# Two-block layer on one core: a modulation batch moved to the ends of the state space groups, and five changes of order in the second block

## The chip, the cores and the metric

The kernel runs on one core of a Trainium2 chip. The metric is the device time of one execution in microseconds; the time of a kernel is the median of its runs.

## The reference

One call computes two transformer-like blocks on a sequence of 256 positions with 2048 features, all in float32. The first block is modulated by a vector `c`: `silu(c) @ w_mod + b_mod` gives six vectors of 2048 that shift, scale and gate. Its mixer joins a dilated attention and a state space branch; then comes a SwiGLU part. The second block has three branches (a linear recurrence with gates, a compressed and windowed attention, an attention with forget gates) and merges them.

```python
mod = (c_act @ w_mod[l] + b_mod[l])[:, None, :]
sh1, sc1, g1, sh2, sc2, g2 = jnp.split(mod, 6, axis=-1)
h = rmsnorm(x, norm1_w[l]) * (1.0 + sc1) + sh1
x = x + g1 * mixer(h, ...)
h = rmsnorm(x, norm2_w[l]) * (1.0 + sc2) + sh2
x = x + g2 * swiglu(h, w_ffn_in[l], w_ffn_out[l])
...
a = jnp.exp(log_a)
drive = jnp.sqrt(-jnp.expm1(2.0 * log_a)) * (inp * uc.astype(jnp.float32))
_, hseq = lax.associative_scan(linear_combine, (a, drive), axis=1)
...
merged = (mg[:, :, 0] * (y_a @ w_branch[l, 0])
          + mg[:, :, 1] * (y_b @ w_branch[l, 1])
          + mg[:, :, 2] * (y_c @ w_branch[l, 2]))
```

## The kernel before

All large products go through TensorE as **chunks**: 16 weight tiles of 128x128 (1 MB), that is one tile of 128 output features over 2048 inputs. There are 544 chunks in one fixed order, in phases with names: `ple`, `qs`, `qkv`, `dt`, `gs`, `ssm0`, `sp0`, `ssm1`, `sp1`, `ap`, `ga`, `wo`, `fi`, `fo` for the first block, `lx`, `lg`, `bf`, `nq`, `cmp`, `bra`, `ng`, `fx`, `brb`, `fg`, `brc`, `w2`, `pg` for the second. `ga`+5 is the sixth chunk of phase `ga`, and `C0["ga"]` is the number of its first.

Every weight is split into an upper and a lower part so that float32 accuracy survives TensorE's reduced format. For chunk c, SyncE loads `raw[c % 4]` as soon as TensorE has used chunk c-4; ScalarE makes the upper half `whi` (line 1088, function `hi`), VectorE the lower half `wlo` (line 1610, function `lo`), both two chunks ahead of TensorE as a rule. TensorE multiplies each tile three times (upper by upper, upper by lower, lower by upper), either as three narrow matmuls of 256 columns (lines 513 to 515) or as one of 512 and one of 256 (508 to 511). Its result is fetched from the accumulator by ScalarE (`take`, line 1098, with an activation function) or VectorE (`add`, line 1620). Every engine runs its own program in the order of the text; only semaphores tie them.

**Modulation.** `w_mod` has 24 batches of 512 columns (order `MORDER`), each of four pieces of 1 MB. Batches from 8 on ride beside other phases by a table: `MPIECE` says after which chunk's load SyncE issues a piece, `MDVE` (two chunks earlier in number, at VectorE's place) when VectorE multiplies and adds it (`mod_piece`, four operations of 128x512, lines 1671 and 1673), `MSUM` after which chunk TensorE sums the batch over the partitions (`mod_block`, eight short matmuls, line 579, waits for `macc_ok`, which VectorE gives by a drain, line 1680), `MDONE` when VectorE adds the bias (`mod_finish`, line 1706). Before, two batches ride in each of `sp0`, `sp1` and `ga`, one in `wo`, four in `fi`.

**State space groups.** `ssm0` and `ssm1` have four groups of ten chunks each. At the end of a group VectorE finishes four tiles (`xs`, `sz`, lines 1964 and 1967) from the products that TensorE makes after the tenth chunk (line 790); ScalarE squares them (line 1298) and TensorE sums the squares (line 744) in the middle of the next chunk.

**Second block.** In `lx` the first four chunks (`leads`) are multiplied before the norm is known; then VectorE rebuilds the input in four quarters: `joined` (line 2204) adds upper and lower part, `normed` (line 2210) scales, ScalarE's `hi_quarter` makes the new upper part, `low_quarter` (line 1768) the new lower part, for which TensorE's next three chunks (`triple`) wait quarter by quarter. `lead_out` (lines 2193 and 2195) and the convolution (lines 2233 and 2236) follow. In `lg`, in two halves i = 0, 1, ScalarE takes eight gates with Silu, and between them Sigmoid, Tanh and Exp (lines 1464 and 1466) and a square root (line 1479) for the recurrence, in the shared buffers `lt` and `la`; a change of function can need a table load. In `bra` the products of the first branch are merged (`branch_post`) while the logits of the first attention batches begin (`att_logits`, line 994); they need `hn_ok`, which VectorE gives after the norm of the compressed keys (lines 1655 to 1659 and 2348). Batch b+1 of the logits waits until VectorE has the maximum of batch b (`att_bias`, line 2368, semaphore `aA`). In `ng` VectorE gates eight tiles (`gated`, lines 2405, 1638, 1640) and computes the forget gates' softplus and their running sum (lines 1719 to 1739, 2438). `brb` is the same as `bra` for the second branch, beside the attention with forget gates (`NSA_B` is its first batch, lines 994 and 997).

Of the kernel before, what the change touches and what calls it, by code (L numbers as in the profile page):

```python
# [12 lines left out]
P = 128  # L13
S = 256
# [59 lines left out]
def first_and_second_block(nc, w16, w11, wm, cst_d, onehot, xt, pt, wab, cw2, out):  # L74
    ctx = ExitStack()
    with ctx:
# [51 lines left out]
        macp = sb("macp", [P, 512], W + 100352)  # L128
        cz = sb("cz", [P, 16, 64], W + 69632)
# [74 lines left out]
        lt = sb("lt", [P, 4, S], W + 8192)  # L204
        LR, LI = ([sb(f"{n}{i}", [P, 4, S], W + o + (24576 if i else 0)) for i in range(2)] for n, o in (("lr", 0), ("li", 4096)))
        la = sb("la", [P, 4, S], W + 98304)
# [178 lines left out]
        MSTAGES = [(0, 13, mraw_a, 4), (13, 15, mraw_b, 4), (15, 17, mraw_b, 4), (17, 20, mraw_w, 2), (20, 24, mraw_c, 2)]  # L385
        MACC = {n: (macc, macp)[n % 2] for n in range(24)}
        MPIECE = {}
        for n0, c0, k, per in ((8, C0["qkv"] + 2, 20, 1.1), (13, C0["sp0"] + 4, 8, 1.4), (15, C0["sp1"] + 4, 8, 1.4), (17, C0["ga"] + 2, 8, 1.4),
                               (19, C0["wo"] + 2, 4, 2), (20, C0["fi"] + 10, 16, 4)):
            for i in range(k):  # L390
                MPIECE.setdefault(c0 + int(i * per), []).append(int(4 * n0) + i)
        MWAIT = {C0["sp0"] + 3: (grp, 5), C0["sp1"] + 3: (grp, 9), C0["fi"] + 3: (used, 2 * C0["fi"])}
        MDVE = {c - 2: ms for c, ms in MPIECE.items()}
        MLAST = {m // 4: c for c, ms in MDVE.items() for m in ms if m % 4 == 3}
        MSUM = {c + 1: n for n, c in MLAST.items()}
# [93 lines left out]
        def _(pe):  # L489
# [338 lines left out]
            for h in range(2):  # L828
# [7 lines left out]
                pe.wait_ge(mod_ok, 15 + 2 * h)  # L836
# [196 lines left out]
            def attention(b0, b1, ph):  # L1033
                att_logits(b0)
                for b in range(b0, b1):
                    if b + 1 < b1:
                        att_logits(b + 1)
                    rides = RIDES.get(b, [])
                    for n in rides[:-1]:
                        branch_chunk(ph, n)  # L1040
# [38 lines left out]
        def _(act):  # L1079
# [228 lines left out]
            for h in range(2):  # L1308
                if h:
                    act.wait_ge(mod_ok, 15)  # L1310
# [143 lines left out]
            for j in range(8):  # L1454
                i = j // 4
                lr, li = LR[i], LI[i]
                c, e = C0["lg"] + j, E0["lg"] + j
                hi(c + 2)
                if j % 4 == 2:
                    act.wait_ge(lru_g, i + 1)  # L1460
                    if i:
                        act.wait_ge(lru_y, 1)
# [5 lines left out]
                take(c, e, gl[:, j, :], ACT.Silu, bias=C("b2", B2["lg"] + j))  # L1468
# [134 lines left out]
        def _(dve):  # L1603
# [294 lines left out]
            def group(i, h, gg):  # L1898
# [25 lines left out]
                for j in range(10):  # L1924
# [8 lines left out]
                    if j < 6:  # L1933
                        convolve(j)
                    if j == 1 and g % 4:
                        norm_scale(g - 1).then_inc(y_sc, 1)
# [260 lines left out]
            def joined(m):  # L2197

                if m % 2:
                    dve.wait_ge(used, 2 * (C0["lx"] + 3) + m // 2 + 1)  # L2200
                else:
                    dve.wait_ge(lead_q, m // 2 + 1)
# [3 lines left out]
            def normed(m):  # L2206

                dve.drain()
                t = wide(m, 4)
                dve.tensor_tensor(accM[:, t, :], accM[:, t, :], wide_rstd, ALU.mult).then_inc(quarter, 1)  # L2210

            lo(C0["lx"] + 4)
            lead_out(0)
            lo(C0["lx"] + 5)
            joined(0)
            normed(0)
            for m in range(4):
                if m < 3:
                    joined(m + 1)
                low_quarter(8 + m, accM)  # L2220
                if m < 3:
                    normed(m + 1)
                if m == 0:
                    lo(C0["lx"] + 6)
# [24 lines left out]
            for i in range(2):  # L2249
                li = LI[i]  # L2250
# [93 lines left out]
            branch_post("a", 1)  # L2344
# [4 lines left out]
            dve.drain().then_inc(hn_ok, 1)  # L2349

# [73 lines left out]
            for t in range(8):  # L2424
                if t != 3:
                    split_lo(C0["ng"] + t + 1)
# [5 lines left out]
                if t == 2:  # L2432
                    split_lo(C0["ng"] + t + 2)
                    softplus(zf[f, :], [sft[f, k, :] for k in (0, 1, 2, 3)], sft[f, 4, :], 4, cut=False)
                    dve.tensor_scalar(sft[f, 4, :], sft[f, 4, :], -1.0, None, ALU.mult)
# [228 lines left out]
```

## Time and profile before

| | us |
|---|---|
| median of 3 runs | 3318.47 (3317.68 to 3318.89) |
| the profiled execution | 3317.84 |
| its span | 3316.0 |
| TensorE busy | 3222.9 (97%) |
| VectorE busy | 2285.1 (69%) |
| ScalarE busy | 1532.5 (46%) |

The page's chain that ended last is 81% TensorE, 9% VectorE, 3% DMA and 3% ScalarE. DMA moved 209 GB/s over the span. In a timeline row, the number in brackets is how long the engine was idle before the row, and what ended that.

### The profile page before, as it was taken

The numbers are of one execution on the slowest core, as the hardware profiler recorded it, in microseconds if no ns is written. First come the engines' busy times: TensorE is split into PE (matmuls) and PEld (weight loads), VectorE is DVE, ScalarE is ACT, GpSimd is POOL, SyncE is SP. The second block draws the span as 40 slices with busy tenths as digits, with TensorE's granted clock in tenths as the row PEclk, the third lists the DMA queues.
The fourth block names the chain that finished last, engine by engine and source line by source line (L and its number), as shares of the span: only waits on it lengthen the run. The fifth ranks groups of instructions, "written<-read, shape, count | busy, mean of one in ns | idle before, by whom it ended". The sixth has DMA issues, their size and how long they took to land.

```text
span 3316.0 us, 52301 instructions
## 1 busy us (share of the span) xinstructions
PE 3222.9 (97%) x22161; PEld 2948.0 (89%) x22161; DVE 2285.1 (69%) x2781; ACT 1532.5 (46%) x1555; POOL 0.2 (0%) x4
## 2 busy tenths in 40 slices
PE   6999999999999999999999999999899999999999
PEld 4888989988998898988888888889899999999987
DVE  5797478877777788777776556766555664555676
ACT  2333555644554334433333333466656474443433
POOL 0000000000000000000000000000000000000000
PEclk9999999999999999999999999999999999999999
DMA  9897545556455686566665566544533444455554
GB/s 374 327 351 271 197 174 182 185 225 234 178 178 193 252 305 241 204 233 236 223 234 200 184 204 202 182 170 170 212 132 139 154 171 147 153 182 210 206 186 157
DMA packets 110413, 693.02 MB, mean 209 GB/s; under 512 B 11519, under 2 KB 18751, under 8 KB 36324
## 3 DMA queue, kind: packets, MB, share of 16 engines
q1 hardware_dynamic: 97776, 655.30, 54.5%
q10 hardware_dynamic: 12404, 34.38, 2.8%
q8 instruction: 175, 2.87, 0.3%
q14 instruction: 58, 0.48, 0.0%
HBM read 679.05 MB, written 13.72 MB: 209 GB/s over the span
## 4 chain that ended last, share of the span: by engine, by line
PE 81%; DVE 9%; DVEq 3%; DMA 3%; ACT 3%; issue 1%; ACTq 0%; SPq 0%
PE accp L508 25%; PE accp L509 14%; PE accp L513 10%; PE accp L515 10%; PE accp L514 10%; DVE wlo L1610 2%; DMA raw<-w 2%; PE accp L511 1%; DVEq L1675 1%; ACT whi L1088 1%; PE pw L589 1%; DVE macc L1673 1%; DVE macp L1673 1%; PE pw L994 1%; PE pw L1029 1%
## 5 line engine op out<-in xcount | busy, mean ns | idle before, releaser
L1610 DVE TENSOR_TENSOR wlo<-raw,whi 128x2048 fp32r<-128x2048 f32 (+1 forms) x544 | 1201.7, 2210 | 530.2 <-ACT whi L1088 525.4
L1088 ACT ACTIVATE whi<-raw 128x2048 fp32r<-128x2048 f32 (+1 forms) x544 | 1002.5, 1847 | 621.0 <-DMA raw<-w 588.5
L508 PE MATMUL accp<-act,whi 128*128 128x512 f32 x2550 | 908.7, 399 | 1.8 <-DVE tf L1620 0.9
L513 PE MATMUL accp<-act,whi 128*128 128x256 f32 x2912 | 844.1, 290 | 12.3 <-ACT gl L1098 5.4
L514 PE MATMUL accp<-act,whi 128*128 128x256 f32 x2912 | 827.9, 284 | 0.0
L515 PE MATMUL accp<-act,wlo 128*128 128x256 f32 x2912 | 827.8, 284 | 0.0
L509 PE MATMUL accp<-act,wlo 128*128 128x256 f32 x2720 | 734.7, 280 | 0.0
L513 PEld LDWEIGHTS accp<-act,whi 128*128 128x128 f32 x2912 | 562.8, 193 | 21.4 <-issue 7.4
L508 PEld LDWEIGHTS accp<-act,whi 128*128 128x128 f32 x2550 | 478.9, 188 | 112.2 <-DVE tf L1620 1.2
L514 PEld LDWEIGHTS accp<-act,whi 128*128 128x128 f32 x2912 | 563.0, 193 | 5.2 <-issue 5.0
L515 PEld LDWEIGHTS accp<-act,wlo 128*128 128x128 f32 x2912 | 562.6, 193 | 0.0
L509 PEld LDWEIGHTS accp<-act,wlo 128*128 128x128 f32 x2720 | 513.1, 189 | 14.7
L508 PE MATMUL accp<-hid,whi 128*128 128x512 f32 x688 | 243.7, 399 | 0.0
L509 PE MATMUL accp<-hid,wlo 128*128 128x256 f32 x704 | 195.1, 281 | 0.0
L508 PE MATMUL accp<-y,whi 128*128 128x512 f32 x450 | 161.7, 401 | 5.0 <-DVE accS L1634 1.8
L508 PEld LDWEIGHTS accp<-hid,whi 128*128 128x128 f32 x688 | 129.3, 188 | 31.4
L1306 ACT ACTIVATE tf<-tf 128x256 f32<-128x256 f32 x42 | 17.6, 418 | 258.3 <-DVE tf L1620 252.0
L509 PEld LDWEIGHTS accp<-hid,wlo 128*128 128x128 f32 x704 | 133.0, 189 | 1.5
L509 PE MATMUL accp<-y,wlo 128*128 128x256 f32 x480 | 129.9, 281 | 0.0
L1098 ACT ACTIVATE tm<-accp,cst 128x256 f32<-128x256 f32 x64 | 30.4, 475 | 183.4 <-PE accp L515 183.2
L513 PE MATMUL accp<-yb,whi 128*128 128x256 f32 x384 | 111.2, 290 | 0.0
L514 PE MATMUL accp<-yb,whi 128*128 128x256 f32 x384 | 109.8, 286 | 0.0
(503 smaller groups left out, 4191.9 us busy)
## 6 DMA issues: line engine op xcount, KB each, us to landing
raw<-w SPq DMA_DIRECT2D x480, 1024.0 KB, 4.8
raw<-w SPq DMA_DIRECT2D x64, 704.0 KB, 4.1
mraw_a<-wm SPq DMA_DIRECT2D x42, 1024.0 KB, 8.6
mraw_b<-wm SPq DMA_DIRECT2D x16, 1024.0 KB, 8.4
mraw_c<-wm SPq DMA_DIRECT2D x16, 1024.0 KB, 6.9
mraw_w<-wm SPq DMA_DIRECT2D x12, 1024.0 KB, 7.0
mraw_x<-wm SPq DMA_DIRECT2D x10, 1024.0 KB, 15.7
acb<-ac_d ACTq DMA_DIRECT2D x8, 1024.0 KB, 4.6
```

What stands on the lines that cost most here:

```text
L508: pe.matmul(acc, wh, both, start=first, stop=False, skip_group_check=True)
L509: mm = pe.matmul(acc[:, 0:S], wl, x2[:, 0, :], start=False, stop=False, skip_group_check=True)
L511: mm = pe.matmul(acc, wh, both, start=first, stop=True, skip_group_check=True)
L513: pe.matmul(acc[:, 0:S], wh, x2[:, 0, :], start=first, stop=False)
L514: pe.matmul(acc[:, 0:S], wh, x2[:, 1, :], start=False, stop=False)
L515: mm = pe.matmul(acc[:, 0:S], wl, x2[:, 0, :], start=False, stop=last)
L589: mm = pe.matmul(pw[64 * (k % 2):64 * (k % 2) + 64, 0, :], cz[:, 4 * j + k, :], mod_slot(4 * n + j)[:, k, :], start=j == j0 and k < 2, sto ...
L994: mm = pe.matmul(o, qq, kk, start=True, stop=kind != 3)
L1029: mm = pe.matmul(o, l, x, start=opens and r == 0 and t == 0, stop=kind >= 2 and t == q and r == 3, skip_group_check=True)
L1088: act.activation(whi[:, c % 4, 0:k, :], raw[:, c % 4, 0:k, :], ACT.Copy).then_inc(hi_done, 1)
L1610: dve.tensor_tensor(wlo[:, c % 4, 0:k, :], raw[:, c % 4, 0:k, :], whi[:, c % 4, 0:k, :].bitcast(F32), ALU.subtract).then_inc(lo_done, 1)
L1673: ins = dve.scalar_tensor_tensor(acc[:, :], src[:, k, :], cact[:, a:a + 1], acc[:, :], ALU.mult, ALU.add)
```

## The change

It has six parts. Batch 13 gets buffers of its own (`mraw_s`, `macs`); its four pieces are loaded and multiplied at the ends of the four groups of `ssm0`, and the batches behind it move up by one, so that `sp0` has 14 and 15, `sp1` 16 and 17, and `ga` only 18, with its pieces three chunks apart. In `lx` the joins are drawn ahead and the wait for TensorE moves from `joined` to `normed`. In `lg` the buffers `lt` and `la` are doubled, the wait for `lru_y` goes, and the take of each third gate stands before Tanh and Exp. In `bra` VectorE norms the compressed keys before `branch_post("a", 1)`. In the attention with forget gates TensorE does one chunk before the second logits. In `ng` the second part of softplus stands behind tile 3, the running sum behind tile 5.

```diff
+        mraw_s = sb("mraw_s", [P, 1, 4, 512], W + 32768)
+        macs = sb("macs", [P, 512], W + 45056)
...
-        lt = sb("lt", [P, 4, S], W + 8192)
+        LT = [sb(f"lt{i}", [P, 4, S], o) for i, o in enumerate((W + 8192, R2 + 28672))]
...
-        la = sb("la", [P, 4, S], W + 98304)
+        LA = [sb(f"la{i}", [P, 4, S], o) for i, o in enumerate((W + 98304, R2 + 16384))]
...
-        MSTAGES = [(0, 13, mraw_a, 4), (13, 15, mraw_b, 4), (15, 17, mraw_b, 4), (17, 20, mraw_w, 2), (20, 24, mraw_c, 2)]
-        MACC = {n: (macc, macp)[n % 2] for n in range(24)}
+        MSTAGES = [(0, 13, mraw_a, 4), (13, 14, mraw_s, 1), (14, 16, mraw_b, 4), (16, 18, mraw_b, 4), (18, 20, mraw_w, 2), (20, 24, mraw_c, 2)]
+        MACC = {n: macs if n == 13 else (macc, macp)[n % 2] for n in range(24)}
...
-        for n0, c0, k, per in ((8, C0["qkv"] + 2, 20, 1.1), (13, C0["sp0"] + 4, 8, 1.4), (15, C0["sp1"] + 4, 8, 1.4), (17, C0["ga"] + 2, 8, 1.4),
+        for n0, c0, k, per in ((8, C0["qkv"] + 2, 20, 1.1), (13, C0["ssm0"] + 11, 4, 10), (14, C0["sp0"] + 4, 8, 1.4), (16, C0["sp1"] + 4, 8, 1.4), (18, C0["ga"] + 2, 4, 3),
...
-        MWAIT = {C0["sp0"] + 3: (grp, 5), C0["sp1"] + 3: (grp, 9), C0["fi"] + 3: (used, 2 * C0["fi"])}
+        MWAIT = {C0["ssm0"] + 3: (dt_ev, 1), C0["sp0"] + 3: (grp, 5), C0["sp1"] + 3: (grp, 9), C0["fi"] + 3: (used, 2 * C0["fi"])}
...
+        MLAST[13] = C0["sp0"] + 2
...
             def attention(b0, b1, ph):
                 att_logits(b0)
                 for b in range(b0, b1):
+                    rides = RIDES.get(b, [])
+                    ahead = 1 if b == NSA_B else 0
+                    for n in rides[:ahead]:
+                        branch_chunk(ph, n)
                     if b + 1 < b1:
                         att_logits(b + 1)
-                    rides = RIDES.get(b, [])
-                    for n in rides[:-1]:
+                    for n in rides[ahead:-1]:
                         branch_chunk(ph, n)
...
-                lr, li = LR[i], LI[i]
+                lr, li, lt, la = LR[i], LI[i], LT[i], LA[i]
                 c, e = C0["lg"] + j, E0["lg"] + j
                 hi(c + 2)
+                take(c, e, gl[:, j, :], ACT.Silu, bias=C("b2", B2["lg"] + j))
                 if j % 4 == 2:
                     act.wait_ge(lru_g, i + 1)
-                    if i:
-                        act.wait_ge(lru_y, 1)
...
-                take(c, e, gl[:, j, :], ACT.Silu, bias=C("b2", B2["lg"] + j))
...
                     if j < 6:
                         convolve(j)
+                    if j == 9:
+                        ride(C0[ph] + 10 * gg + j + 20 * i)
...
             def joined(m):
 
+                t = wide(m, 4)
+                dve.tensor_tensor(accM[:, t, :], act_hi[:, t, :].bitcast(F32), act_lo[:, t, :].bitcast(F32), ALU.add)
+
+            def normed(m):
+
+                dve.drain()
                 if m % 2:
                     dve.wait_ge(used, 2 * (C0["lx"] + 3) + m // 2 + 1)
                 else:
                     dve.wait_ge(lead_q, m // 2 + 1)
...
+            joined(0)
             lo(C0["lx"] + 4)
             lead_out(0)
+            joined(1)
+            joined(2)
+            normed(0)
             lo(C0["lx"] + 5)
...
+            low_quarter(8, accM)
+            normed(1)
+            lo(C0["lx"] + 6)
+            low_quarter(9, accM)
+            normed(2)
+            joined(3)
+            low_quarter(10, accM)
+            normed(3)
+            low_quarter(11, accM)
...
             branch_post("a", 0)
-            branch_post("a", 1)
             dve.wait_ge(kc_ev, 1)
             dve.wait_ge(hr, 7)
             newton(kcs[:, 1, :], kcs[:, 3, :], kcs[:, 4, :])
             dve.scalar_tensor_tensor(kcT[:, :], kcT[:, :], C("gnk"), kcs[:, 1, :], ALU.mult, ALU.mult)
             dve.drain().then_inc(hn_ok, 1)
+            branch_post("a", 1)
...
             for t in range(8):
-                if t != 3:
-                    split_lo(C0["ng"] + t + 1)
+                split_lo(C0["ng"] + t + 1)
...
                 gated("ng", nk, t)
-                if t == 2:
-                    split_lo(C0["ng"] + t + 2)
+                if t == 3:
                     softplus(zf[f, :], [sft[f, k, :] for k in (0, 1, 2, 3)], sft[f, 4, :], 4, cut=False)
+                if t == 5:
                     dve.tensor_scalar(sft[f, 4, :], sft[f, 4, :], -1.0, None, ALU.mult)
```

## Rows read from the trace of the kernel before

**Rows 1.** The page: span, and TensorE's busy time and instructions.

```profile
span 3316.0 us, 52301 instructions
PE 3222.9 (97%) x22161; PEld 2948.0 (89%) x22161; DVE 2285.1 (69%) x2781; ACT 1532.5 (46%) x1555; POOL 0.2 (0%) x4
```

**Rows 2.** Waits of TensorE: line, waited for, us in total, times, longest.

```profile
PE accp L513 <- ACT gl L1098: 5.4, 2, 4.0
...
PE pw L579 <- DVEq L1680: 4.3, 3, 2.5
PE pw L994 <- DVE nmx L2368: 4.1, 2, 3.3
...
PE pw L994 <- DVEq L2349: 3.4, 1, 3.4
...
PE accp L513 <- DVE wlo L1610: 2.3, 2, 2.1
```

**Rows 3.** Windows: stretch, busy us (instructions) by engine, TensorE clock, DMA share, GB/s.

```profile
1203.30:1210.70 7.40, 7.40 (x37) 7.40 (x38) 6.80 (x11) 0.84 (x1) 0.00 (x0) 0.54 0.57 236
2196.00:2200.90 4.90, 4.90 (x43) 4.90 (x42) 3.25 (x4) 3.10 (x3) 0.00 (x0) 1.00 0.44 187
2226.40:2231.30 4.90, 4.88 (x23) 4.88 (x24) 3.11 (x2) 3.41 (x3) 0.00 (x0) 0.50 0.05 18
2406.00:2412.20 6.20, 6.18 (x21) 5.46 (x22) 2.29 (x2) 5.78 (x7) 0.00 (x0) 0.50 0.00 0
2617.00:2620.40 3.40, 3.40 (x18) 3.40 (x17) 3.16 (x5) 0.00 (x0) 0.00 (x0) 0.50 0.17 70
2784.30:2787.70 3.40, 3.38 (x17) 3.38 (x17) 0.00 (x0) 3.40 (x9) 0.00 (x0) 0.51 0.00 0
```

**Rows 4.** Timelines of three engines at the first group end in `ssm0`: start, us, what.

```profile
498.42 0.48 DVE L1964 SCALAR_TENSOR_TENSOR xs<-xs,cst,pw 128x256 f32<-128x256 f32 x1 [3.26 <-PE pw L790]
...
502.11 0.42 ACT L1298 ACTIVATE dec<-sz 128x256 f32<-128x256 f32 x1 [0.47 <-DVE sz L1967]
...
504.55 0.81 PE L744 MATMUL pw<-dec,ones 128*128 128x256 f32 x3
```

**Rows 5.** Line 441, the modulation loads, from issue to landing, over the whole span.

```profile
DMA to landing us min/median/max: 6.4/8.2/24.6
```

**Rows 6.** Timeline of VectorE in `ga`: one modulation piece.

```profile
1199.97 3.22 DVE L1673 SCALAR_TENSOR_TENSOR macp<-mraw_w,cact,macp 128x512 f32<-128x512 f32 x4
```

**Rows 7.** Timeline of VectorE in `lx`: first and last `low_quarter`, first convolution.

```profile
2139.30 1.23 DVE L1768 TENSOR_TENSOR act<-accM,act 128x1024 fp32r<-128x1024 f32 x1
...
2152.43 1.22 DVE L1768 TENSOR_TENSOR act<-accM,act 128x1024 fp32r<-128x1024 f32 x1 [1.13 <-ACT act L1135]
...
2158.64 0.41 DVE L2233 TENSOR_SCALAR uc<-ub,cst 128x256 f32<-128x256 f32 x1
```

**Rows 8.** Timeline of ScalarE in the second half of `lg`.

```profile
2214.75 1.97 ACT L1088 ACTIVATE whi<-raw 128x2048 fp32r<-128x2048 f32 x1
2219.86 1.71 ACT L1464 ACTIVATE lt<-lr,lcon 128x256 f32<-128x256 f32 x4 [3.14 <-DVE yb L1640]
2221.58 1.28 ACT L1466 ACT_TABLE_LOAD   x1
...
2226.26 1.90 ACT L1088 ACTIVATE whi<-raw 128x2048 fp32r<-128x2048 f32 x1
```

**Rows 9.** Timelines of ScalarE and VectorE in `bra`: the keys' root, and `bra`+3.

```profile
2398.71 0.23 ACT L1111 ACTIVATE kcs<-kcs 128x30 f32<-128x30 f32 x1
...
2400.78 2.29 DVE L1610 TENSOR_TENSOR wlo<-raw,whi 128x2048 fp32r<-128x2048 f32 x1 [11.37 <-ACT whi L1088]
```

**Rows 10.** Timeline of VectorE in `ng`: softplus begins, and the lower half of `ng`+6.

```profile
2602.77 0.28 DVE L1723 TENSOR_SCALAR sft<-sft 8x256 f32<-8x256 f32 x1
...
2613.19 2.28 DVE L1610 TENSOR_TENSOR wlo<-raw,whi 128x2048 fp32r<-128x2048 f32 x1
```

**Rows 11.** Timeline of VectorE in `brb`: the lower half of `brb`+2.

```profile
2791.57 2.28 DVE L1610 TENSOR_TENSOR wlo<-raw,whi 128x2048 fp32r<-128x2048 f32 x1
```

More of the change, by code:

```diff
@@ L835, in _ @@
                 eight(f"sp{h}", ys, j0=3)
-                pe.wait_ge(mod_ok, 15 + 2 * h)
+                pe.wait_ge(mod_ok, 16 + 2 * h)
             for c in range(4):
@@ L1309, in _ @@
                 if h:
-                    act.wait_ge(mod_ok, 15)
+                    act.wait_ge(mod_ok, 16)
                 for i in range(0, 2):
@@ L2203, in joined @@
                 t = wide(m, 4)
-                dve.tensor_tensor(accM[:, t, :], act_hi[:, t, :].bitcast(F32), act_lo[:, t, :].bitcast(F32), ALU.add)
-            def normed(m):
-                dve.drain()
-                t = wide(m, 4)
                 dve.tensor_tensor(accM[:, t, :], accM[:, t, :], wide_rstd, ALU.mult).then_inc(quarter, 1)
+            joined(0)
             lo(C0["lx"] + 4)
             lead_out(0)
+            joined(1)
+            joined(2)
+            normed(0)
             lo(C0["lx"] + 5)
[L2215 to L2224, printed above, removed]
+            low_quarter(8, accM)
[7 more added lines that the diff above has]
+            low_quarter(11, accM)
             for _ in range(2):
@@ L2249, in _ @@
             for i in range(2):
-                li = LI[i]
+                li, lt, la = LI[i], LT[i], LA[i]
                 dve.wait_ge(lru_g, i + 1)
```

## The prediction

> **What bounds the kernel now.** I read the page's table of engines first. TensorE is busy for 97% of the span of 3316.0 us [rows 1], so the kernel can only get shorter where TensorE stands still or runs slowly. The second view is the list of what TensorE waited for: few and short waits, and the diff touches the places of five of its largest groups [rows 2]. The third is the windows by clock. Right behind several of these waits the granted clock falls to 0.5, which is 1.2 GHz; elsewhere it is 1.0, 2.4 GHz [rows 3]. At the full clock 4.9 us hold 43 narrow matmuls, at half clock 23: in 4.9 us some 20 matmuls of 0.12 us are lost, 2.4 us. So a wait can cost its idle time and then about half of the slow stretch behind it. Last come the timelines of VectorE and ScalarE at the places of the diff [rows 4 to 11].
>
> A full chunk (48 narrow matmuls at 0.12, or 16 times 0.24 + 0.12) is 5.76 us. The program is one chain of such chunks, and each weight load is released by TensorE's use of a chunk four back, so I let a gain at one place carry to the end unless a later row shows VectorE or ScalarE late there.
>
> **Part by part.** I take the six edits in order of time.
>
> *Modulation.* Before, `ga` carries two batches, eight pieces. VectorE spends 3.22 us on a piece [rows 6], and with the lower half and the gate work it needs about 7.5 us for a chunk with a piece and 4.3 us for one without, against 5.76. Twice `mod_block` is ready too late; with a third small wait that is 4.3 us, the longest 2.5 [rows 2], and the two in `ga` I put at 4.1. Behind the first lie 7.4 us at a clock of 0.54 with 37 matmuls [rows 3], where the full clock would hold about 65: 28 times 0.12 are 3.3, of which I take 2.9, since some are the short ones of the block. After, `ga` has four pieces, three chunks apart. VectorE regains 1.5 us in each chunk without a piece, so the one block left there finds its sum ready. The other block moves to `sp0`+3 (eight short matmuls, 0.9 us of TensorE at 0.12 each); there TensorE waits for the lower half of the weights anyway, so 0.9 is saved as well. Sum 7.9 us.
>
> The price is in `ssm0`. At each of the four group ends VectorE now also does a piece, in the place where it idles 3.26 us before the first `xs` step [rows 4]. The piece takes 3.2: it fits with nothing to spare. If it is 1 us late, `xs`, `sz` and ScalarE's four squares behind it are 1 us late; they end at 502.53 and TensorE takes them at 504.55 [rows 4], so 2.0 us are free. The piece is fetched behind the weight load that SyncE issues when `ssm0`+7 is used; from there to `xs` are two chunks with the small matmuls of the group, 13.7 us, so 10.5 to VectorE's arrival. The median landing is 8.2 [rows 5]. SyncE's new wait (`dt_ev`, once, queued ahead of the load of `ssm0`+4) is over when that load may start. I take 0.2 us in all, bounds 0 and 4. Net **7.7**.
>
> *Joins (`lx`).* Before, the first quarter goes through `joined`, `normed`, ScalarE's copy and, after another `joined`, `low_quarter` at 2139.30; each of these 128x1024 operations takes 1.2 us [rows 7]. After, three joins run while VectorE waits for other things, and `normed(0)` starts when TensorE has passed k=3 of the last lead, one chunk before the end of the leads at 2138.1 plus 1.4: 2133.8. It ends at 2135.0, the lower half of `lx`+5 ends at 2137.3, `low_quarter` follows there: 2.0 earlier. From the first `low_quarter` to the last, before took 13.1 us [rows 7]; after it is seven such operations of 1.2, one lower half of 2.3 and one ScalarE copy of 1.1: 11.9, so 3.2 earlier at the last one. Behind it lie the same three leads, lower half and first convolution [rows 7], on which TensorE's chunk `lx`+7 waits. I take **3.2**, bounds 1 (the weights of `lx`+6 late) and 4.
>
> *Roots and takes (`lg`).* The removed waits: 5.4 us in two [rows 2], and 2.4 us of half clock behind the second [rows 3], 7.8 at most. ScalarE does not get all that. The Silu take now stands before Tanh and Exp, and the next Silu comes after Exp, so at least one more table load per half is needed, 1.28 us [rows 8]; whether Tanh needs one of its own after Silu no row shows (after Sigmoid it needs none). In the first half the take moved ahead saves TensorE's 1.5, while the `whi` behind is where it was (0.15 later). In the second half ScalarE ends the upper half of `bf` at 2216.7 [rows 8]; then load 1.28, take 0.47, Tanh 1.71, load 1.28, Exp 1.71, and the upper half of `nq`+0 starts at 2223.2 instead of 2226.26 [rows 8]. The 3.14 us for `lru_y` are gone (two buffers), two table loads stand in their path. VectorE's chain to `nq`+3 (lower halves, square, root, scans, four outputs) hangs on that `whi` and moves by the same 3.1, and TensorE, which would otherwise gain more, waits for it in pieces of 1 to 2 us at `bf`, `nq`+1 and `nq`+3. I take **3.0**; with a second extra load per half 2.6 less (0.4), with no clock drop and no wait behind, 7.8.
>
> To the table loads: the rows show 1.28 us from start to the next ACTIVATE. The Trainium skill (ScalarE: Activation LUTs, "What ACT_TABLE_LOAD costs" and "Rules for kernel authors") has about 2.66 us for each switch with its drain, and tells to do all of one set before switching, which this edit does not. By its figure the edit would give 2.8 us less; the trace disagrees, since every load here is followed by its ACTIVATE after 1.28 to 1.30 us.
>
> *Compressed keys first (`bra`).* ScalarE has the root at 2398.94, but VectorE sits in the lower half of `bra`+3 until 2403.07 [rows 9], and the first logits wait 3.4 us [rows 2]. After, the four small steps end at about 2400.1 and the logits start when the chunk ends, at 2400.8. VectorE is then in that same lower half, behind which the mask and maximum of batch 0 are queued (to 2403.9), and the logits of batch 1 wait for them: 2.0 us idle instead of 3.4 + 0.8. They start at 2403.9 instead of 2406.0: 2.1. Before, the 6.2 us from there ran at 0.50 with 21 matmuls [rows 3]; the eight of 256 columns took 3.2 us where 1.7 do at full clock, the rest loses 1.3. All of it back gives 4.9; one slow stretch behind the 2.0 us takes 1.5 of it. I take **4.2**, bounds 2 and 5.
>
> *Forget chain (`ng`).* Before, softplus, scan and a gated output stand between 2602.77 and the lower half of `ng`+6 at 2613.19 [rows 10], for which TensorE waits 2.1 us [rows 2]; then 18 matmuls in 3.4 us at half clock [rows 3] where 30 would go, 1.4. After, the gated output of tile 3 (1.3 us) and softplus (7.7) stand there, and scaling and scan (1.4) go behind the next lower halves, which are then two chunks ahead. The lower half starts 1.3 earlier, so TensorE waits 0.9, and waits of that size have no slow clock behind them in this trace. **2.7**, bounds 1.3 and 3.5.
>
> *Fox attention (`brb`).* The second logits wait 3.3 us for the first ones' maximum [rows 2] and then run at half clock: 17 in 3.4 us [rows 3], 1.7 more than at full clock. After, a whole chunk (5.8) lies between, which covers the wait. Behind it VectorE's mask, scale and the lower half of `brb`+2, before at 2791.57 [rows 11], move to 2792.1 and end at 2794.4, where TensorE arrives at 2794.2: 0.2 lost. **4.8**, bounds 3 and 5.
>
> Sum: 7.7 + 3.2 + 3.0 + 4.2 + 2.7 + 4.8 = 25.6 us. The profiled execution took 3317.84 (its span and 1.8 around it); less 25.6 it is 3292.2. The median of the runs shown is 0.6 above it, so I forecast **3292.9 us**. With all low bounds the sum is 3.5 + 1 + 0.4 + 2 + 1.3 + 3 = 11.2, with all high ones about 33.
>
> **The rivals.** *A: waits come back.* TensorE would arrive earlier at places where VectorE or ScalarE have little slack (`bf`, `nq`, `bra`+4, `sp0`), and a new idle time of 2 us can bring the slow clock back. For it speaks that `nq` and `bra` already leave 2 us in my count. Then the gain is the sum of low bounds to some 18: about 3303.
>
> *B: the table loads.* Two more per half in `lg`, or one that costs more than its row: 2.6 us less, 3295.5. Only the missing row for Tanh after Silu speaks for it.
>
> *C: nothing is won.* The idle time is small because engines are balanced, and each freed microsecond is spent at the next wait: 3316.
>
> *D: slower, through the group ends.* The four pieces stand in VectorE's order ahead of the `xs` steps, and a late piece holds everything. VectorE arrives about 10.5 us after the issue and 2.0 are free behind, so landings up to 12.5 cost nothing. To be slower than before by 6.6 us the four would have to lose 32 us, 8 each, that is land after 20.6 us. The longest modulation load landed after 24.6, the median after 8.2 [rows 5], and the long ones are in the opening, where DMA is full. From 18.9 us of landing time on the whole gain is spent, and at 20.6 the time is 3325.
>
> **How the numbers follow.** Forecast 0.58, A 0.22, B 0.11, C 0.05, D 0.04. The forecast's own range is 3286 to 3299 (each term with half its bounds, and clock stretches elsewhere that may fall otherwise). A's times reach to 3307; with C and D out, 8 in 10 lie in 3286 to 3306. A measurement of this kernel can tell about 0.2% (6.6 us) from no change. All of forecast and B and nearly all of A are more than that: faster 0.91; C is the same, 0.05; D slower, 0.04.
>
> **What the profile after would show.** In TensorE's waits no `mod_block` wait above 1 us in `ga`; the wait for the maximum in `brb` gone; the one for `hn_ok` gone with some 2 us at the logits of batch 1; about 1 us for the lower half in `ng`. In the windows the slow stretches of `ga`, `lg`, `ng` and `brb` gone. In VectorE's timeline `xs` at the `ssm0` group ends directly behind the pieces, ScalarE's squares still 2 us before TensorE's sum. Two more table loads in `lg`, each 1.28. The prediction is wrong if slow stretches turn up in other places of the second block, if `sp0` waits longer by the moved block, or if the group ends show waits for a piece.

## The result, and the profile after

The kernel after took **3290.88 us** (median of 4 runs, 3288.90 to 3296.48), the kernel before beside it 3318.68; the ratio is 0.992, 95% interval 0.9908 to 0.9932. Timed a second time (`after_again`, below) it took 3289.58, ratio 0.9917 (0.9902 to 0.9932). The forecast was 3292.9. The gain is 27.8 us where 25.6 was worked out.

The page of after, the lines that answer to [rows 1]: TensorE is 10.0 us less busy on the same number of matmuls (22161), and ScalarE has two instructions more.

```profile
span 3294.7 us, 52303 instructions
PE 3212.9 (98%) x22161; PEld 2938.4 (89%) x22161; DVE 2286.1 (69%) x2781; ACT 1535.2 (47%) x1557; POOL 0.2 (0%) x4
```

TensorE's waits in after (line, waited for, us in total, times, longest), which answer to [rows 2]:

```profile
PE accp L516 <- DVE wlo L1614: 4.7, 6, 1.5
...
PE pw L997 <- DVE nmx L2377: 2.2, 1, 2.2
...
PE accp L516 <- ACT ub L1104: 1.4, 1, 1.4
...
PE pw L582 <- DVEq L1684: 0.7, 2, 0.4
```

The 4.3 us for `mod_block` are 0.7, the 3.4 for `hn_ok` and the 3.3 for the maximum in the Fox attention (the one with forget gates, beside `brb`) are gone. The 5.4 for `gl` are gone too; in their place TensorE waits 3.6 us for VectorE's lower halves, in four pieces of at most 1.5 (the other two of the six pieces, 0.9 and 0.2, lie in `ng` and elsewhere). New in the list is 2.2 for `nmx` at the logits of batch 1, which the forecast had put at 2.0.

The windows of after at the places of [rows 3] (stretch, PE, PEld, DVE, ACT, POOL busy with instructions, TensorE's clock, DMA share, GB/s), and below them two in the unchanged attention of branch `a`:

```profile
1204.70:1212.10 7.40, 7.40 (x64) 7.40 (x64) 5.93 (x9) 3.42 (x4) 0.00 (x0) 1.00 0.62 216
2215.60:2220.50 4.90, 4.90 (x42) 4.90 (x43) 3.06 (x2) 4.85 (x7) 0.00 (x0) 1.00 0.49 197
2393.40:2399.60 6.20, 6.04 (x50) 5.80 (x48) 5.35 (x13) 4.14 (x3) 0.00 (x0) 1.00 0.00 0
2601.00:2604.40 3.40, 3.40 (x31) 3.40 (x30) 3.16 (x5) 0.30 (x1) 0.00 (x0) 1.00 0.60 251
2763.50:2766.90 3.40, 3.40 (x30) 3.37 (x29) 2.93 (x6) 0.00 (x0) 0.00 (x0) 1.00 0.00 0
2544.00:2547.40 3.40, 3.40 (x18) 3.40 (x18) 1.39 (x7) 3.39 (x9) 0.00 (x0) 0.51 0.14 55
2554.30:2557.70 3.40, 3.40 (x18) 3.40 (x17) 0.87 (x5) 3.39 (x10) 0.00 (x0) 0.50 0.36 149
```

All five stretches at half clock (1.2 GHz; I call them slow stretches) of [rows 3] are at the full clock in this execution: 64 matmuls instead of 37 in the same 7.4 us in `ga`, 50 instead of 21 in 6.2 in `bra`. The last two rows are the other side: at the end of branch `a` before had one such stretch, behind a wait of 1.95 us; this execution of after has another one ahead of it, behind a wait of 1.04.

**Where the time went, by stage.** Both programs send TensorE the same weight matmuls in nearly the same order. So I took the start of the same matmul in two timelines and how far it stands ahead of before. The table gives what each stage adds to that lead. The two columns of after are its two profiled executions (3296.48 and 3287.95 us; before's took 3317.84).

| stage | forecast | after | `after_again` |
|---|---|---|---|
| up to `ssm0` (unchanged code) | 0 | -3.1 | 0.4 |
| `ssm0` to the start of `ga` | -0.2 (cost) | -1.0 | -0.4 |
| `ga` | 7.9 | 8.5 | 8.5 |
| `lx` | 3.2 | 2.6 | 3.3 |
| `lg`, to `nq`+3 | 3.0 | 3.9 | 3.9 |
| to the start of `bra` | 0 | 0.1 | 1.5 |
| `bra`, two chunks | 4.2 | 5.3 | 5.0 |
| attention of branch `a` | 0 | -1.6 | -0.2 |
| `ng` | 2.7 | 2.9 | 2.8 |
| `brb` | 4.8 | 4.7 | 4.7 |
| all between and behind these | 0 | -0.9 | 0.4 |
| sum | 25.6 | 21.4 | 29.9 |

The stages that the diff touches repeat within 0.7 us. The row `bra` holds more than its edit. Before has one more slow stretch, at the very start of `bra` and ahead of everything that the edit moves, behind a wait of 2.0 us (`pw` L965 for ScalarE's `hct`, in unchanged code). Its window in before, then the same place in after:

```profile
2384.90:2388.30 3.40, 3.40 (x18) 3.39 (x17) 2.84 (x2) 2.07 (x2) 0.00 (x0) 0.50 0.53 224
2374.30:2377.70 3.40, 3.40 (x30) 3.39 (x29) 2.84 (x2) 2.07 (x2) 0.00 (x0) 1.00 0.70 284
```

In both executions of after TensorE waits less at that place (1.5 and 1.7 us) and has no slow stretch there, which is worth 1.5 us. From the second chunk of `bra` to the fourth the lead grows by 4.0 in after and 3.5 in `after_again`. Without that 1.5 the stages that the diff touches add up to 25.4 and 26.3, against 25.6 in the forecast.

The two executions differ by 8.5 us, most of it where the code is the same: 3.5 before `ssm0`, 1.4 at the end of `cmp`, 1.4 in the attention of branch `a`, 1.3 in the last row.

### The profile page after: what moved, and what is told of

The parts are those of the page before. It is cut to its first block, busy times and chain, and to the rows that moved or that the text cites. A ratio compares the mean times of both kernels' runs of the same rounds, so it can differ in the third digit from the quotient of the medians.

```text
span 3294.7 us, 52303 instructions
## 1 busy us (share of the span) xinstructions
PE 3212.9 (98%) x22161; PEld 2938.4 (89%) x22161; DVE 2286.1 (69%) x2781; ACT 1535.2 (47%) x1557; POOL 0.2 (0%) x4
## 4 chain that ended last, share of the span: by engine, by line
PE 83%; DVE 8%; DMA 3%; DVEq 2%; ACT 2%; issue 1%; ACTq 0%; SPq 0%
PE accp L511 26%; PE accp L512 14%; PE accp L516 11%; PE accp L517 11%; PE accp L518 11%; DVE wlo L1614 3%; DMA raw<-w 2%; PE accp L514 2%; ACT whi L1094 1%; DVE macc L1677 1%; DVEq L1679 1%; PE pw L592 1%; PE pw L1032 1%; PE pw L997 1%; DMA mraw_a<-wm 0%
## 5 line engine op out<-in xcount | busy, mean ns | idle before, releaser
L516 PE MATMUL accp<-yb,whi 128*128 128x256 f32 x384 | 110.5, 288 | 0.2 <-DVE wlo L1614 0.2
L518 PE MATMUL accp<-yb,wlo 128*128 128x256 f32 x384 | 109.2, 284 | 0.0
```

Of the source, the lines that this page charges most:

```text
L516: pe.matmul(acc[:, 0:S], wh, x2[:, 0, :], start=first, stop=False)
L518: mm = pe.matmul(acc[:, 0:S], wl, x2[:, 0, :], start=False, stop=last)
```

## The experiments

**The modulation alone (`mod_alone`).** The kernel before with only the first of the six parts:

```diff
+(13, 14, mraw_s, 1), (14, 16, mraw_b, 4), (16, 18, mraw_b, 4), (18, 20, mraw_w, 2)
+                    if j == 9:
+                        ride(C0[ph] + 10 * gg + j + 20 * i)
```

> The kernel before with the modulation part of the change alone. My theory (two late sums in ga, and the half clock behind the first): 7.7 us less than before, about 3311.0 by the medians, with ga shorter by 8 and sp0 and ssm0 together longer by less than 1. Rival A (the work meets the next wait in sp0 and ssm0): 4 us less, 3314.7. Rival D (a late piece holds the group end): slower than before.

Measured: 3308.60, ratio 0.9974 (0.9964 to 0.9984), that is 8.6 us (5.3 to 11.9) less than before. In its profile `ssm0` costs 0.2, `sp0` 0.5, `ga` gives 8.5 (0.58 us ahead of before at its start, 9.05 at `ga`+11), and the lead stays at 8.5 to 9.3 until the last stage. So this part is worth what it was put at, and a lead won in the first block is carried through some 2000 us.

**Wait and clock apart (`filler`, `filler_half`).** Do the slow stretches cost time of their own? Matmuls that nobody reads stand ahead of six waits of the kernel before, so that TensorE is not idle there:

```diff
+            def filler(n, bank):
+                for _ in range(n):
+                    pe.matmul(pw[:, bank, 0:S], ones[:, :], C("tri", 0, S), start=True, stop=True)
```

> The kernel before, with matmuls that nobody reads (256 columns each) put ahead of six waits: 10 and 5 ahead of the two modulation sums in ga, 15 ahead of bf, 13 ahead of the first logits of bra, 8 ahead of ng+6, 13 ahead of the second logits of brb. They are shorter than the waits, so TensorE has work while it would be idle and its next matmul comes no earlier. If the half clock behind these waits comes from TensorE standing still, and costs what I counted (2.9 + 2.4 + 3.0 + 1.4 + 1.7), the kernel is about 11 us faster than before, 3307, with the granted clock at 1.0 in all five places. If only the idle time counts, the time is that of before, or some us above it.

Measured: 3314.79, ratio 0.999 (0.9981 to 0.9999), some 3 us less, not 11. Ten of the fillers took 4.5 us instead of 2.2, each of them being two records:

```profile
1202.19 4.49 PE L585 MATMUL pw<-cst,ones 128*128 128x256 f32 x20
1206.51 0.95 PE L579 MATMUL pw<-ones,macp 128*128 128x1 f32 x8
```

(start, duration, instruction; `ga`.) They overran a wait of 2.5 us, so the run showed only that the slow stretches at these places go when TensorE is kept busy (one of 3.4 us turned up in `lx`, behind a wait of 2.5, where before has the wait and no slow stretch). `filler_half` has about half as many:

> The kernel before with unread matmuls ahead of six waits, as in filler, but about half as many (5 and 3 in ga, 9 at bf, 7 at each attention place, 4 at ng+6), since in filler each of them took two passes of 0.21 us and 10 of them 4.5 us, longer than the waits that they were to fill. Nothing else differs from the kernel before. Theory (behind each of these waits a stretch at half clock costs time of its own): the waits end when they did and the stretches behind them run at full clock, 2.9 us in ga, 1.3 in bra, 1.4 in ng and 1.7 in brb; the 2.4 at bf are spent again at nq+3, which waits for VectorE. 7.3 us less than the kernel before, 3311. Rival 1: the fillers again delay what follows by as much as the clock gives back, 3315. Rival 2: with waits only partly filled the slow stretches stay, and the time is that of the kernel before.

Measured: 3312.76, ratio 0.9988 (0.9979 to 0.9997), 4 us less (1 to 7); in its profile the lead over before is 5.6 at the last stage, in it are `ng` 1.5 (1.4 expected), `fx` to `brb` 1.6 (1.7), `bra` 3.0 (1.3), `lg` 0.7 (0), `ga` a loss of 1.5 (a gain of 2.9 expected), the end of branch `a` a loss of 1.5 to a second slow stretch; the rest lies in unchanged code. Of the 3.0 in `bra`, 1.5 is before's slow stretch at its start (above), whose place lies 11 us ahead of the unread matmuls. From the second chunk on TensorE first gains 2.9, what the whole slow stretch behind the first logits costs, and then gives back 1.1 by a longer wait for VectorE's `accM` (1.52 us against 0.42), so 1.8 are left. In `bra`, `ng` and `brb` theory holds: the clock is a cost of its own. In `ga` it is not, as TensorE's waits between 1190 and 1260 us show, first before's, then those of `filler_half`:

```profile
PE pw L579 <- DVEq L1680: 4.0, 2, 2.5
```

```profile
PE pw L579 <- DVEq L1694: 3.6, 2, 3.3
```

At full clock TensorE came to the second `mod_block` earlier and waited 3.3 us there instead of 1.6: VectorE sets the pace through the whole of `ga`, and what the clock gives back is spent waiting. And this longer wait had a slow stretch behind it:

```profile
1239.70:1243.10 3.40, 3.40 (x19) 3.40 (x18) 3.31 (x5) 0.00 (x0) 0.00 (x0) 0.50 0.00 0
```

(the columns of the windows above). Rival 2 is out, theory holds in `bra`, `ng` and `brb`, and in `ga` the clock's time was given back as rival 1 says, but to VectorE's lateness and not to the fillers.

**The takes and the chunk in the Fox attention put back (`undo_lg_brb`).** The kernel after, the doubled `lt` and `la` kept:

```diff
-                    ahead = 1 if b == NSA_B else 0
+                    ahead = 0
...
-                take(c, e, gl[:, j, :], ACT.Silu, bias=C("b2", B2["lg"] + j))
                 if j % 4 == 2:
...
+                take(c, e, gl[:, j, :], ACT.Silu, bias=C("b2", B2["lg"] + j))
```

> The kernel after, with the takes of lg back behind Tanh and Exp (the doubled buffers and the missing wait for lru_y stay) and the chunk of brb back behind the second logits. For brb 4.8 us are lost. For lg I now expect that the doubled buffers carry nearly all: the upper half of nq+0 starts at the same time with either order, so 0 to 1 us are lost, in all 5.3: 3296.2. The rival (the takes, moved ahead of Tanh and Exp, are half of the gain of lg): 2 us more, 3298.2.

Measured: 3295.93, ratio 0.9932 (0.9918 to 0.9947), 5 to 6 us above the kernel after. By stage: `lg` gives 3.95 over before with the old order of the takes and 3.93 with the new. The new order does save 1.7 us in the first half of `lg`, where TensorE's wait of 1.46 for the take is back in `undo_lg_brb`, but at `nq`+1 both kernels are level: there TensorE waits 1.5 us for the lower half with the new order and 0.7 with the old. So the whole gain of `lg` is the doubled buffers', and the two additional table loads cost nothing that the stage shows. In `brb` the lead shrinks by 1.2, where after gains 4.7: 5.9 us for that one chunk, 1.1 more than the 4.8 of the forecast. The windows of `undo_lg_brb` and of before over the second logits say why:

```profile
2764.80:2771.60 6.80, 6.03 (x28) 6.03 (x29) 2.70 (x9) 3.87 (x9) 0.00 (x0) 0.50 0.00 0
```

```profile
2784.30:2791.10 6.80, 6.78 (x44) 6.78 (x45) 2.82 (x11) 3.87 (x9) 0.00 (x0) 0.75 0.00 0
```

At the same place of the program the clock was at half for all of 6.8 us here and for half of them in before, behind the same wait of 3.29 us. A restored wait does not always restore the same slow stretch.

**The other three put back (`undo_lx_bra_ng`).** The kernel after with before's order of joins, compressed keys and forget chain:

```diff
-            joined(1)
-            joined(2)
-            normed(0)
...
+            branch_post("a", 1)
             dve.wait_ge(kc_ev, 1)
...
-                if t == 5:
```

> The kernel after, with the joins of lx, the order of the compressed keys in bra and the forget chain of ng as before. By the terms of the sum 3.2 + 4.2 + 2.7 = 10.1 us are lost: 3301.0. If the gains of one place were spent at the next wait (rival A), less than 6 would be lost: under 3297.

Measured: 3299.14, ratio 0.9945 (0.993 to 0.9959), 8.3 us above the kernel after. By stage the lead grows by 0.1 in `lx` (after: 2.6 and 3.3), 0.8 in the two chunks of `bra` (5.3 and 5.0), 1.5 in `ng` (2.9 and 2.8), and as in after in `lg` (3.9) and `brb` (4.7). So the edit in `lx` is worth 2.5 to 3.2, that in `bra` 4.2 to 4.5, that in `ng` 1.2 to 1.4 and not 2.7. The 1.5 of the lead in `ng` that comes without the edit is before's slow stretch behind `ng`+6: this kernel has the same wait of 2.1 us there and no slow stretch. The 0.8 in `bra` are the 1.5 of before's slow stretch at its start, less 0.7. The 8.3 lie between the 10.1 of the terms and the 6 of rival A.

**How much room the group ends have (`late1`, `late2`).** Rival D, the one that would have made the kernel slower, hangs on two numbers, 10.5 us from issue to VectorE's arrival and 2.0 behind. These two kernels fetch the pieces later and change nothing else:

```diff
+        for _k in range(4):
+            _c = C0["ssm0"] + 11 + 10 * _k
+            MPIECE[_c].remove(52 + _k)
+            MPIECE.setdefault(_c + 1, []).append(52 + _k)
```

> The kernel after, with one edit: at each of the four ssm0 group ends the piece of the modulation weights is fetched one chunk later (behind the next weight load that SyncE issues); VectorE's order is the same, so it meets the piece at the same place. By my count a landing up to 12.5 us after the issue costs nothing (10.5 until VectorE arrives, 2.0 free behind); one chunk later is 5.8 us later, so a median landing of 8.2 comes 3.5 us after VectorE's arrival and 1.5 us beyond the slack. Theory (the place is tight, every late microsecond beyond 2.0 is paid): 4 times 1.5 = 6 us more than the kernel after. Rival (the slack is larger than I counted, or loads land sooner there): within 1 us of the kernel after. VectorE's timeline should show an idle time ahead of each piece in either case.

> As late1, but the piece is fetched two chunks later at the first three group ends and one later at the last. Theory: a landing of 8.2 us then comes 9.3 us after VectorE's arrival, 7.3 beyond the slack, so 3 times 7.3 + 1.5 = 23 us more than the kernel after: about 3314, nearly the whole gain of the change spent. Rival (larger slack S instead of 2.0): 3 times (9.3 - S) and nothing for the last; with S = 5, 13 us. late1 and late2 together give S and the landing time: the difference between them should be three times a chunk, 17 us, once both are beyond the slack.

Measured: `late1` 3293.01, ratio 0.9927 (0.9909 to 0.9945), 2 to 3 us above the kernel after; `late2` 3317.05, ratio 0.9995 (0.9986 to 1.0004), 26 us above it: the whole gain spent. First, the first group end in after (compare [rows 4]): VectorE's timeline, then ScalarE's, then the landing of the four loads over the whole span:

```profile
498.63 0.48 DVE L1675 TENSOR_SCALAR macs<-mraw_s,cact 128x512 f32<-128x512 f32 x1
499.18 2.40 DVE L1677 SCALAR_TENSOR_TENSOR macs<-mraw_s,cact,macs 128x512 f32<-128x512 f32 x3
501.96 0.48 DVE L1970 SCALAR_TENSOR_TENSOR xs<-xs,cst,pw 128x256 f32<-128x256 f32 x1 [0.38 <-PE pw L793]
```

```profile
505.65 0.42 ACT L1304 ACTIVATE dec<-sz 128x256 f32<-128x256 f32 x1 [0.47 <-DVE sz L1973]
```

```profile
DMA to landing us min/median/max: 6.7/7.5/8.2
```

SyncE issued the piece at 488.65 and VectorE came for it at 498.63, 10.0 later, with no idle time before it. Behind it `xs` even waited 0.38 us for TensorE: the piece fits into the gap. The last square ends at 506.07, and TensorE takes the first of the four at 508.09, 2.0 later. So a landing is free up to 10.0 + 0.4 + 2.0 = 12.4 us; the forecast had 12.5. VectorE's timeline at the same place in `late1`, then in `late2`, and of `late2` TensorE's timeline and the line of its waits:

```profile
499.00 0.49 DVE L1679 TENSOR_SCALAR macs<-mraw_s,cact 128x512 f32<-128x512 f32 x1 [2.77 <-DMA mraw_s<-wm]
```

```profile
507.54 0.49 DVE L1679 TENSOR_SCALAR macs<-mraw_s,cact 128x512 f32<-128x512 f32 x1 [11.27 <-DMA mraw_s<-wm]
```

```profile
512.15 1.22 PE L751 MATMUL pw<-dec,ones 128*128 128x256 f32 x2 [6.33 <-ACT dec L1308]
```

```profile
PE pw L751 <- ACT dec L1308: 17.1, 3, 6.3
```

In `late1` VectorE waits 12.9 us for the four pieces (2.8, 2.8, 4.5 and 2.8). 2.4 of each is free, so 3.3 in all should be paid; measured in the stage 2.7, most of it (2.0) at the third end, whose piece came latest. By the times alone `late1` can't be told from the kernel after (its four runs lie between 3289.20 and 3298.72). Expected were 6, because I had taken the landing at 8.2, the median over all modulation loads [rows 5], and here it was 6.9. In `late2` VectorE waits 11.3, 10.8 and 9.6 us for the first three pieces. 11.27 less 2.4 is 8.9; the three ends cost 9.3, 8.1 and 7.6, sum 25.0, of which 17.1 is idle and 7.9 the work behind it, where the clock is at half. The window over the first of them:

```profile
505.00:530.00 25.00, 18.67 (x90) 15.14 (x89) 20.24 (x33) 11.68 (x20) 0.00 (x0) 0.80 0.38 140
```

(in after 144 matmuls stand in the same 25 us at a clock of 1.00). Theory holds: the slack was 12.4 where 12.5 stood, split as 10.0 + 0.4 + 2.0 and not as 10.5 + 2.0. Rival D is a true mechanism: with three of the four loads issued some 12.7 us later (counted from VectorE's arrival) it takes all of the gain. In the kernel after the loads land 1.8 to 3.3 us ahead of VectorE (10.0 less 8.2 and 6.7).

**Further on the same way (`next_lg`, `next_all`, `after_again`, `next_all_again`).** What is left in `lg` of after are three waits for VectorE's lower halves (1.2 at `bf`, 1.5 at `nq`+1, 0.7 at `nq`+3). ScalarE's second half of `lg` in after:

```profile
2210.13 1.28 ACT L1104 ACT_TABLE_LOAD   x1
2211.43 0.48 ACT L1104 ACTIVATE gl<-accp,cst 128x256 f32<-128x256 f32 x1
2211.80 1.70 ACT L1469 ACTIVATE lt<-lr,lcon 128x256 f32<-128x256 f32 x4
2213.50 1.28 ACT L1471 ACT_TABLE_LOAD   x1
2214.79 1.71 ACT L1471 ACTIVATE la<-lr,lcon 128x256 f32<-128x256 f32 x4
2216.41 1.90 ACT L1094 ACTIVATE whi<-raw 128x2048 fp32r<-128x2048 f32 x1
```

The upper half at 2216.41 needs nothing of the five instructions above it. It is a copy of 1.9 us; the 0.47 to 1.1 us in the expectation below are not its time. `next_lg` draws it ahead of them:

```diff
-                hi(c + 2)
+                if j % 4 != 3:
+                    hi(c + 2)
...
                 if j % 4 == 2:
+                    hi(c + 3)
```

> The kernel after, with one edit: in each half of lg the upper half of the weights that stood behind Tanh and Exp on ScalarE goes ahead of them (one chunk further ahead than before), so that ScalarE's 0.47 to 1.1 us copy no longer stands behind two functions and two table loads. Theory (TensorE's remaining 1.2 us at bf and 1.5 at nq+1 wait for that upper half): 1 to 2 us less than the kernel after. Rival (the chain on VectorE, lower halves, square, scans and outputs, sets nq+3): the idle time moves from bf to nq+3 and the time is that of the kernel after within 1 us.

> next_lg with two more edits: in lx the first convolution goes ahead of the last lower half and that lower half ahead of the last three leads (TensorE's chunk lx+7 waits 1.4 us behind that convolution); in bra VectorE takes the masks and maximum of batch 0 ahead of the closing work of branch a's tile 1, so that the logits of batch 1, for which TensorE idles 2.2 us, start sooner. Theory: 0.9 us in lx and 1.2 in bra on top of next_lg, 2 to 4 us less than the kernel after. Rival (each wait is handed to the next place, here the accumulator's release at bra+4 and the lower half of lx+7): within 1 us of the kernel after, or slower.

Measured: `next_lg` 3285.16, ratio 0.9904 (0.9889 to 0.9919); `next_all` 3283.57, ratio 0.9901 (0.9886 to 0.9915). `next_lg` gains more than theory's 1 to 2: its stage `lg` is 4.1 us shorter than after's, the three waits (3.4) and a little more. TensorE's waits from 2150 to 2270 us, in after and in `next_lg`:

```profile
PE accp L516 <- DVE wlo L1614: 3.6, 4, 1.5
```

```profile
PE accp L516 <- DVE wlo L1616: 0.2, 1, 0.2
```

I had thought of the wait at `nq`+3 as VectorE's own chain; it was late only because its upper half was. The two other edits of `next_all` did what theory says: the one in `lx` gave 1.6 at `lx`+7, of which 1.2 are left at `nq`+3 (0.9 expected), the one in `bra` 1.4 (1.2 expected; the wait for `nmx` is 0.9 instead of 2.2). By the medians they add 1.6 us to `next_lg`, a difference smaller than the intervals. Beside after on one chip:

> The kernel after, unchanged, timed on the same chip as next_all_again. Its profiled execution was 5 us above the median of its own runs, with 3 us of it in the unchanged opening. Expected: ratio to the kernel before 0.992, about 3291; the stages from ssm0 on as in the first profile within 0.5 us each, except the attention of branch a, where one or two stretches at half clock can fall (1.5 us).

> next_all, unchanged, beside the kernel after on one chip. Theory (its three edits shorten three waits and nothing behind them gives it back): 5 to 7 us below after_again, ratio to the kernel before 0.990. Rival (the difference between the two earlier measurements was the chip's): within 2 us of after_again.

Measured: 3289.58 (ratio 0.9917, 0.9902 to 0.9932) and 3284.55 (0.9903, 0.9887 to 0.992). The difference of the medians is 5.0 us, as theory has it, though the two intervals overlap; the four runs of `next_all` (3282.41 to 3286.85) lie all below the four of after (3287.95 to 3292.34). It is the fastest version that ran.

## Why the prediction was right, step by step

*The bound.* That TensorE's gaps and half-clock stretches are all there is to gain held: in after's first profile the span is 21.3 us shorter, 10.0 of it less busy time on the same matmuls (the slow stretches) and 11.3 less idle time.

*Modulation, 7.7; 7.5 and 8.1 by the stages of after, 8.6 (5.3 to 11.9) by the times.* The sum was right, one argument in it was not. I added 2.9 for the clock as a cost beside the waits. `filler_half` shows that in `ga` the clock alone gives nothing: with it restored, the next `mod_block` waits as much longer. What is left as the cause is that VectorE has four pieces less there, 12.9 us of its work. That is reached by exclusion: no run takes the pieces away and leaves the block. So the step on the clock failed, and that the sum came out near 7.9 all the same is in part luck. The price in `ssm0` is 0.0 to 0.4 where 0.2 stood. The moved block in `sp0` costs 0.4 to 0.6 where it was put at nothing. TensorE's waits around it, first before's, then after's:

```profile
PE accp L508 <- DVE wlo L1610: 0.8, 1, 0.8
```

```profile
PE pw L582 <- DVEq L1684: 0.4, 1, 0.4
```

The wait for the lower half is gone, as forecast, but the block waits 0.4 for its own sum: the cover was there, and the block came too early to use all of it. The low bound of this part is 7.9 less 4, 3.9, and not the 3.5 in the sum of low bounds; nothing else hangs on it.

*Joins, 3.2; 2.6 and 3.3.* The edit carries 2.5 to 3.2 by the undo. In after the first `low_quarter` came 1.4 us earlier than in before (counted from the stage's start), not 2.0, and the last one 2.6.

*Roots and takes, 3.0; 3.9.* The step that the upper half of `nq`+0 starts 3.1 earlier measured 3.25. That the Silu takes, with their table loads, had a part in it failed: the doubled buffers alone give the same. And I let VectorE's chain set `nq`+3, though the chain itself hung on that upper half; `next_lg` took 4 us more out of this place. On the rule of the Trainium skill that I weighed (ScalarE: Activation LUTs, "Rules for kernel authors": all of one set before the next): the two added loads are in the count (1557 instructions against 1555), each takes 1.28 to its ACTIVATE as above, and the order with more switches was as fast as the one with fewer (3.93 against 3.95). The predicted loss of 2.8 by the page's figure did not show. Tanh after Silu had no load of its own (2211.80 above), so rival B fell.

*Compressed keys, 4.2; 5.3 and 5.0 by the stage, 4.0 and 3.5 without before's slow stretch at its start; the edit carries 4.2 to 4.5 by the undo.* The logits of batch 1 waited 2.2 us where I had 2.0. My working gives two numbers, 4.9 if no slow stretch comes behind that wait and 3.4 if one does, and the 4.2 is a value between them that fits neither. In the first execution of after none came: TensorE was 5.1 ahead, and then gave 1.1 back by a wait of 1.5 us for VectorE's `accM` (at the place that rival A calls `bra`+4), which the sum did not have; 4.0 was left. In the second (`after_again`) one came and nothing was given back, 3.5. The clock's part was sized rightly: 1.5 + 1.3 = 2.8 in the working, 2.9 in `filler_half` before the same 1.1 is given back. Other kernels with this order had it otherwise: `undo_lg_brb` had 6.8 us at half clock behind the same 2.2 us, and only 2.2 of gain.

*Forget chain, 2.7; 2.9 and 2.8.* The wait fell to 0.9 us with no slow stretch behind it, as forecast. But with the edit undone the stage still gained 1.5, with no slow stretch in it, though the wait stood as before. The shorter wait is the edit's (1.2 of the 2.7); that the slow stretch hangs on the length of the wait is not shown, and its 1.5 can also go without the edit.

*Fox attention, 4.8; 4.7.* The chunk stands between the two logits, and `brb`+2 is late by what was forecast.

*The rivals.* A (waits come back): they did at `bf` and `nq` in the sizes that the sum already had, and at `bra`+4 for 1.1 us that it had not, and no more. B and C are out. D is shown as a mechanism by `late2`, and the place at which it decides is as worked out: 12.4 us against 12.5, and 25 us lost over three ends by pieces that land 19.6 to 21.3 us after the issue of the kernel after.

*The signs of being wrong.* Of the three that the forecast names, one did show, and small: a slow stretch at a new place (the end of branch `a`, 1.5 us, in one of two executions). `sp0` doesn't wait longer (2.0 us in all against 2.3), and no group end waited for a piece. Before's slow stretch at the start of `bra` is the other way round, 1.5 us of gain that the forecast had no term for. So the nearness of 27.8 to 25.6 is in part luck: the touched stages without it are 25.4 and 26.3, with single stages off by up to 0.9, and in `ng` 1.5 that the edit isn't shown to carry.

**What stays open.** Where a slow stretch falls and how long it lasts isn't settled: in one execution of after a wait of 1.04 us at the end of branch `a` has one behind it, in the other it has none. So what an edit gains by the clock at one place holds for the executions that were profiled, and every stage number here comes from one or two of them. In `bra` 0.7 us that the undone kernel loses against before was not followed up. The first 440 us of after's first profile are 3.5 us longer on the same code than those of the second; 2.9 of it lie at one place near 340 us, where TensorE waits 3.6 us for `nmx` (L1848) with a slow stretch behind it, and 2.1 us without one in the second. Why that wait differs is open.

## What to carry to other kernels

Count the waits of the bounding engine and the slow stretches behind them as one sum only where the releasing engine has room; where that engine itself is late (VectorE in `ga`), taking work from it is what helped here, and clock and wait came back together. When a step is queued behind functions that it does not need, look for the copy that stands there before calling the chain behind it the bound. Compare a stage's gain with the same edit undone: in `ng` and at the start of `bra` 1.5 us each would otherwise have been booked to edits that had no part in them. For work put into another engine's gap, write down two numbers, from issue to the meeting and from there to the next taker, and try them by issuing later: here one chunk later cost 2.7 us and two chunks later everything.

## What the runs showed of the hardware

The same wait of TensorE can have a slow stretch behind it or not. Of the 13 profiles of this case, the wait of 1.95 us at the end of branch `a` has one in 12 (all but `next_all`), the wait of 1.04 us ahead of it in four (after, `filler_half`, `next_lg`, `next_all`). The wait of 2.22 us at the logits of batch 1 has one in four of six (`after_again`, `late1`, `late2`, and `undo_lg_brb`, there for 6.8 us), and none in after and `next_lg`. The 2.1 us in `ng` have one in before and `mod_alone`, and none in `undo_lx_bra_ng`. In `late2` the clock fell at each of the three waits of 4.7 to 6.3 us. The forecast took waits of 0.9 us as harmless for the clock; that held in `ng`. Keeping TensorE busy with unread matmuls (`filler`) took the slow stretches away at the places where they stood. An fp32 matmul of 256 columns with fp32 operands came as two records 0.21 us apart, 0.43 us of TensorE, where I had counted one. A table load took 1.28 us, and the ACTIVATE behind it started 1.29 to 1.30 us after the load did. Two profiled executions of one kernel differed by 8.5 us, of which 3.5 lay in the opening and most of the rest at places where a slow stretch fell or did not.
